# Small matmuls placed in separate row and column groups of the array, and the squares taken as the query units leave the array

## The reference

```python
for l in range(DEPTH):                                   # DEPTH = 2, 512 tokens, width 1024
    h = rms_norm(x, norm1_g[l]) * (1.0 + sc1) + sh1
    gq, gk, gv, glr, gr, sq, sk, sv, ga, gb = split(h @ w_in[l])
    ya = gla_branch(gq, gk, gv, glr, gr, ...) @ w_up_a[l]
    yb = swa_branch(sq, sk, sv, ..., rel_bias) @ w_up_b[l]
    x = x + g1 * ((sigmoid(ga) * ya + sigmoid(gb) * yb) @ w_out[l])
    ...                                                  # PEER: the larger part of the time, untouched
# gla_branch: 4 heads, chunks of 64 tokens, state S of 128 x 256 for each head
def step(S, inp):
    o = where(causal, q_dec @ k_inv.T, 0) @ v + q_dec @ S
    S = S * exp(b_last) + k_tail.T @ v
# swa_branch: 16 query heads, 2 key heads of 64, window 128
q = rms(q over 64) * qn_g / 8;  k = rms(k over 64) * kn_g
logits = q @ k.T + bias[bucket(distance)]                # then softmax with a sink, and @ v
```

## Time and profile before

| what | value |
|---|---|
| median of 3 runs | 4279.65 us |
| the profiled execution, whole | 4281.71 us |
| its span | 4279.9 us, mean granted clock of TensorE 0.967 |
| busy share: PE, DVE, POOL, ACT | 95%, 66%, 43%, 36% |
| chain that ended last | PE 77%, issue 10%, DVE 6%, ACT 3%, POOL 3%, DMA 1% |
| start, to the first unit | 0 to 62.06 us |
| GLA loop of layer 0 | 229.5 to 346.5 us |
| from its end to the head loop | 346.5 to 405.3 us |
| the same two stretches of layer 1 | 2345.3 to 2459.2 and 2459.2 to 2516.5 us |

### The profile page before, as it was taken

How to read it: one execution, slowest core, us unless ns; L and a number is a source line. 1 busy time by engine, 2 the same in 40 slices (tenths; PEclk the granted TensorE clock), 3 DMA queues, 4 the chain that set the end, 5 groups by cost and what they waited for, 6 DMA issues and landing times.

```text
span 4279.9 us, 49995 instructions
## 1 busy us (share of the span) xinstructions
PE 4056.3 (95%) x18106; PEld 3279.2 (77%) x18106; DVE 2821.2 (66%) x4282; ACT 1530.1 (36%) x2219; POOL 1845.6 (43%) x956
## 2 busy tenths in 40 slices
PE   6899998998999999999998999989899999999999
PEld 4666876886877887888876668778778778788887
DVE  3124754698988946888733156247988989378786
ACT  2434523343333333333335255233333333333332
POOL 2321223344444446777423212333344444487772
PEclk9998989999999999999999998999999999999999
DMA  6434975243445459999934358463334544699996
GB/s 246 143 116 145 329 268 201 81 143 113 170 158 201 167 206 333 382 347 349 314 127 140 103 200 301 158 194 106 125 128 179 189 159 169 239 373 372 351 350 210
DMA packets 411891, 918.72 MB, mean 215 GB/s; under 512 B 38544, under 2 KB 176560, under 8 KB 410064
## 3 DMA queue, kind: packets, MB, share of 16 engines
q1 hardware_dynamic: 328080, 664.83, 44.8%
q0 software_dynamic: 45056, 134.38, 8.6%
q10 hardware_dynamic: 38592, 117.46, 7.0%
HBM read 793.85 MB, written 256.90 MB: 246 GB/s over the span
## 4 chain that ended last, share of the span: by engine, by line
PE 77%; issue 10%; DVE 6%; ACT 3%; POOL 3%; DMA 1%; SPq 1%; POOLq 0%; ACTq 0%; DVEq 0%
PE ps L887 13%; PE ps L888 13%; PE ps L889 13%; PE ps L902 10%; PE ps L903 10%; PE ps L904 10%; POOL w_lo L841 3%; PE ps L1185 2%; PE ps L1074 1%; PE ps L1059 1%; PE ps L1019 1%; DMA raw<-in_stream_dram 1%; ACT w_hi L519 1%; DVE raw L1263 1%; PE ps L1082 1%
## 5 line engine op out<-in xcount | busy, mean ns | idle before, releaser
L841 POOL TENSOR_TENSOR w_lo<-raw,w_hi 128x1024 fp32r<-128x1024 f32 x440 | 1133.5, 2577 | 2076.0 <-ACT w_hi L519 2076.0
L519 ACT ACTIVATE w_hi<-raw 128x1024 fp32r<-128x1024 f32 x504 | 534.2, 1060 | 1873.0 <-PE ps L889 1397.2
L887 PE MATMUL ps<-h_hi,w_hi 128*128 128x512 f32 x2880 | 1146.0, 398 | 7.9 <-DVE idxT L1522 7.8
L888 PE MATMUL ps<-h_hi,w_lo 128*128 128x512 f32 x2880 | 1137.3, 395 | 0.0
L889 PE MATMUL ps<-h_lo,w_hi 128*128 128x512 f32 x2880 | 1134.8, 394 | 0.0
L887 PEld LDWEIGHTS ps<-h_hi,w_hi 128*128 128x128 f32 x2880 | 550.3, 191 | 130.7 <-issue 17.4
L889 PEld LDWEIGHTS ps<-h_lo,w_hi 128*128 128x128 f32 x2880 | 547.8, 190 | 120.1
L888 PEld LDWEIGHTS ps<-h_hi,w_lo 128*128 128x128 f32 x2880 | 549.0, 191 | 107.9
L854 POOL DMA_INDIRECT down<-expert_down,e_row x256 | 336.3, 1314 | 216.6 <-DVE ps L1647 95.9
L1594 DVE TENSOR_TENSOR hot_i<-same_i,pick 128x1024 fp32r<-128x1024 f32 x192 | 421.5, 2195 | 0.0
L846 POOL DMA_INDIRECT acts<-expert_act,e_act x256 | 375.5, 1467 | 104.1 <-issue 77.4
(11 more groups left out here) (255 smaller groups left out, 6048.2 us busy)
## 6 DMA issues: line engine op xcount, KB each, us to landing
raw<-in_stream_dram SPq DMA_DIRECT2D x648, 512.0 KB, 3.4
expert_down<-in_stream_dram SPq DMA_DIRECT2D x256, 512.0 KB, 5.9
expert_act<-gel ACTq DMA_DIRECT2D x256, 256.0 KB, 2.0
raw_more<-in_stream_dram SPq DMA_DIRECT2D x128, 512.0 KB, 6.8
expert_gate<-gatebuf ACTq DMA_DIRECT2D x12, 4096.0 KB, 12.5
a_in<-expert_act SPq DMA_DIRECT2D x128, 384.0 KB, 6.6
g_in<-expert_gate SPq DMA_DIRECT2D x128, 384.0 KB, 8.2
ada_first<-in_stream_dram SPq DMA_DIRECT2D x16, 512.0 KB, 12.6
```

What stands on the lines that cost most here:

```text
L519: return act.activation(o, i, ACT.Copy)
L841: pool.tensor_tensor(w_lo[:, s, :], raw[:, b, :], w_hi[:, s, :].bitcast(F32), ALU.subtract).then_inc(lo_ready, 1)
L887: pe.matmul(o, w_hi[:, s, w], mov_hi[:, c, :], start=c == 0, stop=False)
L888: pe.matmul(o, w_lo[:, s, w], mov_hi[:, c, :], start=False, stop=False)
```

## The change

Four edits.

1. **Bands.** `rel` and `onehot` are loaded four times, to partitions 0, 32, 64 and 96, by eight small transfers instead of two. Head h's matmul uses the 32 rows from 32 (h mod 4), and six PSUM banks instead of two.
2. **State updates.** One call now makes the products of both chunks of a tile for two heads, the even chunk on rows 0 to 63 into bank 4, the odd chunk on rows 64 to 127 into bank 5; the second call, for the other two heads, follows the first unit. There are three states instead of two, and VectorE updates both chunks before the mean squares of the output.
3. **Squares.** ScalarE takes the square of a query or key unit straight from PSUM when it copies the unit out, into six buffers. TensorE sums them inside the GLA loop, four to a bank, each into 32 partitions of its own (32 columns of the array). The reciprocal and the root follow in the last tile, on 128 partitions.
4. **Root spreads.** Each uses 32 rows and one of six banks; keys first. Four stand ahead of unit `U_MIXA + 2`, four behind it, the last two (queries of heads 12 to 15) behind `U_MIXA + 3`. `bias_free` is raised once the root is there.

```diff
+BAND_BANKS = (0, 1, 4, 5, 6, 7)
+ROOTS = (8, 9, 0, 1, 2, 3, 4, 5, 6, 7)
+ROOT_BANKS = (4, 5, 6, 7, 2, 3)
...
+    state_2 = at("state_2", 88.5, [P, GH, DV])
-    inv_rms = at("inv_rms", Z + 92, [20, SEQ])
-    spread = at("spread", Z + 98, [20, 10 * P])
+    inv_rms = at("inv_rms", Z + 110, [P, SEQ])
+    spread = at("spread", Z + 104, [P, 3, P])
+    squares = [at(f"square{b}", Z + kb, [P, SEQ]) for b, kb in enumerate((64, 66, 68, 70, 96, 110))]
...
+        def state_at(c, h):
+            return state[:, c % 3, h, :] if c % 3 < 2 else state_2[:, h, :]
...
# SyncE: the constants
-            sp.dma_start(rel[:], rel_in).then_inc(consts_loaded, 16)
-            sp.dma_start(onehot[:], onehot_in).then_inc(consts_loaded, 16)
+            for g in range(4):
+                r = slice(32 * g, 32 * g + 32)
+                sp.dma_start(rel[r], rel_in).then_inc(consts_loaded, 16)
+                sp.dma_start(onehot[r], onehot_in).then_inc(consts_loaded, 16)
...
# ScalarE
+            def square(l, m):
+                t = m - U_SQ
+                if t >= 6:
+                    act.wait_ge(sq_mm, l * 10 + t - 5)
+                act.activation(squares[t % 6][:], ps[:, ORDER[m] % 2, :], ACT.Square).then_inc(sq_ready, 1)
...
+                elif m in range(U_SQ, U_SV):
+                    square(l, m)
+                    column_out(l, m, qT_s[:, m - U_SQ, :] if m < U_SK else kT_s[:, m - U_SK, :])
...
-                transposed_hi(oa_hi, l * 2 * KC)
-                square(0)
-                for t in range(1, 10):
-                    square(t)
-                after_unit(l, U_MIXA)
                 act.wait_ge(sq_inv, l + 1)
                 act.activation(inv_rms[:], inv_rms[:], ACT.Sqrt).then_inc(sq_root, 1)
+                act.wait_ge(sq_mm, (l + 1) * 10)
+                transposed_hi(oa_hi, l * 2 * KC)
+                after_unit(l, U_MIXA)
                 after_unit(l, U_MIXA + 1)
...
# TensorE: band
             for h in range(SH):
-                if h >= 2:
-                    pe.wait_ge(band_out, h - 1)
-                pe.matmul(ps[:, h % 2, 0:384], rel[:, h:h + 1].to_broadcast([32, P]), onehot[:], start=True, stop=True
-                          ).then_inc(band_mm, 1)
+                if h >= len(BAND_BANKS):
+                    pe.wait_ge(band_out, h - len(BAND_BANKS) + 1)
+                r = slice(32 * (h % 4), 32 * (h % 4) + 32)
+                pe.matmul(ps[:, BAND_BANKS[h % len(BAND_BANKS)], 0:384], rel[r, h:h + 1].to_broadcast([32, P]), onehot[r],
+                          start=True, stop=True).then_inc(band_mm, 1)
...
# TensorE: GLA loop over p
+                def updates(l, p, half):
+                    n = l * 2 * TT + 2 * p + half
+                    if n:
+                        pe.wait_ge(state_ready, n)
+                    for h in (2 * half, 2 * half + 1):
+                        for e in range(2 if p < TT - 1 else 1):
+                            r = slice(64 * e, 64 * e + 64)
+                            mm = pe.matmul(ps[:, 4 + e, h % 2 * 256:h % 2 * 256 + 256], ktail[r, h, p, :],
+                                           v_g[r, p, h * DV:(h + 1) * DV], start=True, stop=True)
+                    mm.then_inc(upd_mm, 1)
...
-                    for e in range(2):
-                        c = 2 * p + e
-                        if e:
-                            unit(l, U_SQ + 3 * p)
-                        if c == 7:
-                            break
-                        if c:
-                            pe.wait_ge(state_ready, l * 7 + c)
-                        r = slice(64 * e, 64 * e + 64)
-                        for h in range(GH):
-                            mm = pe.matmul(ps[:, 4 + h // 2, h % 2 * 256:h % 2 * 256 + 256], ktail[r, h, p, :],
-                                           v_g[r, p, h * DV:(h + 1) * DV], start=True, stop=True)
-                        mm.then_inc(upd_mm, 1)
+                    updates(l, p, 0)
+                    unit(l, U_SQ + 3 * p)
+                    updates(l, p, 1)
                     for m in range(U_SQ + 3 * p + 1, min(U_SQ + 3 * p + 3, U_MIXA)):
                         unit(l, m)
+                    for t in range(max(4 * p - 4, 0), min(4 * p, 10)):
+                        pe.wait_ge(sq_ready, l * 10 + t + 1)
+                        r, w = 32 * (t % 4), C_HEADS + 18 - 2 * (t // 4)
+                        pe.matmul(ps[r:r + 32, 7, :], const[:, w:w + 32], squares[t % 6][:], start=t < 4, stop=t >= 6,
+                                  skip_group_check=True).then_inc(sq_mm, 1)
                     pe.wait_ge(attn_ready, k + 1)
-                    pe.wait_ge(state_ready, l * 7 + 2 * p + 1)
+                    pe.wait_ge(state_ready, l * 2 * TT + 2 * p + 2)
...
# TensorE: after the loop
-                for t in range(10):
-                    pe.wait_ge(sq_ready, l * 10 + t + 1)
-                    w = C_HEADS + 18 - 2 * t
-                    pe.matmul(ps[0:20, 2, :], const[:, w:w + 20], tmp[:, t % 2, :], start=t == 0, stop=t == 9
-                              ).then_inc(sq_mm, 1)
...
-                for t in range(10):
-                    if t >= 2:
-                        pe.wait_ge(sqk_ready, l * 10 + t - 1)
-                    pe.matmul(ps[:, 2 + t % 2, :], spread[:, t * P:t * P + P], inv_rms[:], start=True, stop=True
-                              ).then_inc(root_mm, 1)
-                pe.wait_ge(sqk_ready, (l + 1) * 10)
+                def roots(first, last):
+                    for n in range(first, last):
+                        t = ROOTS[n]
+                        if n >= 6:
+                            pe.wait_ge(sqk_ready, l * 10 + n - 5)
+                        r = slice(32 * (t % 4), 32 * (t % 4) + 32)
+                        pe.matmul(ps[:, ROOT_BANKS[n % 6], :], spread[r, t // 4, :], inv_rms[r], start=True, stop=True).then_inc(root_mm, 1)
...
+                roots(0, 4)
+                unit(l, U_MIXA + 2)
+                roots(4, 8)
+                pe.wait_ge(sqk_ready, l * 10 + 8)
                 logits(0)
-                unit(l, U_MIXA + 2)
                 unit(l, U_MIXA + 3)
+                roots(8, 10)
+                pe.wait_ge(sqk_ready, l * 10 + 10)
                 for h in range(SH):
...
# VectorE: GLA loop
+                def update(p, half):
+                    dve.wait_ge(upd_mm, l * 2 * TT + 2 * p + half + 1)
+                    if p:
+                        dve.wait_ge(o_mm, l * TT + p)
...
-                    update(2 * p)
+                    update(p, 0)
+                    update(p, 1)
+                    if p == TT - 1:
+                        dve.wait_ge(sq_mm, (l + 1) * 10)
+                        step(dve.tensor_scalar(inv_rms[:], ps[:, 7, :], EPS, None, ALU.add))
+                        dve.reciprocal(inv_rms[:], inv_rms[:]).then_inc(sq_inv, 1)
...
-                    if p < TT - 1:
-                        update(2 * p + 1)
...
# VectorE: after the loop
                 gated_a(l, 0)
-                dve.wait_ge(sqk_ready, (l + 1) * 10)
+                dve.wait_ge(sq_root, l + 1)
                 dve.sem_inc(bias_free, 1)
...
+                rooted(0, 8)
...
                     if h == 0:
+                        rooted(8, 10)
                         dve.wait_ge(silu_ready, l + 2)
```

78 lines of the change are left out of this document (34 added, 44 removed).

## The result

The changed kernel takes 4222.45 us (median of 4 runs, 4219.56 to 4226.69), the kernel before 4277.74 on the same chip (4272.71 to 4283.12): a ratio of 0.9871, 95% interval 0.9854 to 0.9888. Forecast was 4214, range 4197 to 4243. When the pair was timed again the ratio was 0.9828 (0.9794 to 0.9863); the kernel before read higher then (4295.07) and the changed one the same (4223.60).

What follows compares the result with a forecast made beforehand. TensorE, busy or waited for throughout, was taken as the bound. Start 5.0 plus 2 x (GLA loop 17 + between loops 18.0 - head loop 4.3) = 66.4 off 4281.7 gave 4215.3, by the median 4214; range 4197 to 4243.

Steps and rivals of the forecast that it cites:

- Rows side by side: Array row groups: matmuls on different row groups overlap fully, plus 0.25 us per burst.
- GLA loop: Loop of each layer: paired updates halve bursts and waits for VectorE go, 17 us less a layer.
- Between the loops: Stretch from GLA loop to head loop: 40.7 us against 58.8, 18.0 less in each layer.
- Start: Up to the first unit: bands side by side, but data lands late; 5.0 us gained, bounds -2.7 to +7.5.
- The four blocks: Start: last four blocks of `ada_first`, queued behind the band stores, land near 44 us; dot products end at 50.6.
- 5.0 of 6.3: Start: of 6.3 us, 5.0 counted, since the second `w_lo` now falls beside the norm's work.
- One is lengthened as now: Start: one VectorE dot product stretched from 1.22 to 3.37 us while GpSimd works on `w_lo` beside it.
- Head loop: Gives back 4.3 us a layer: wait of 2.7 at head 1 and 1.6 for half clock behind it.
- The chain to head 1: Head loop: late buffers, load, ScalarE's copy, table load and exponentials end 13.2 us after its begin; TensorE wants them at 10.5.
- no overlap: Rival, whole change: row groups don't overlap, nor four column groups more than now; 27 us gained, 4253; chance 0.09.
- Lateness: Rival, head loop: buffers stay late through twelve heads, 52 us a layer lost, 4309; chance 0.03.
- The ring as pace maker: Rival: weight buffers, not TensorE, tie the head loop; between the loops only 7.9 gained a layer, 4225; chance 0.12.

Runs made afterwards that it cites:

- updates alone: The kernel before with only the state-update edit (chunks paired on row groups, third state, VectorE updating both chunks ahead of the normaliser): 4244.27 us, ratio 0.9895.
- the stores moved: Changed kernel with six root spreads ahead and early dot products, plus band stores put behind all sixteen loads of `ada_first`: 4200.35 us, ratio 0.9772.
- the weights ahead of them: As the kernel with the stores moved, but band stores also behind the first four weight blocks and the parameter rows: 4206.80 us, ratio 0.9815.
- early dot products: Changed kernel with head 0's two dot products ahead of VectorE's last two multiplications by the root: 4214.14 us, ratio 0.9828.
- Six spreads ahead: Changed kernel with six root spreads in one stretch, the last four behind head 0's logits, and early dot products: 4204.08 us, ratio 0.9791.

## Why the prediction was right, and where it was not

- **Rows side by side**: right, and the size too. Forecast 1.15 for an update burst and 1.1 for one of four squares; measured 1.14 and 1.06.
- **GLA loop**: right in its size (17 against 18.7 and 15.7), incomplete in its cause. The prediction put the end of the waits down to the new pairing ("the products of p wait only for the update of p - 1"). The runs split layer 0 so: 11.8 from moving VectorE's update ahead of the normaliser (move alone); 10.5 from pairing on rows with what was left of the waits (105.2 to 94.7, updates alone); 3.5 back for the squares (94.7 to 98.2). In layer 1: 10.2, 9.1 and 3.5. Taken in this sequence, over half of the gross gain is an order on VectorE that needs no row groups. It stands in the diff, and I walked past it, because I priced without asking what VectorE did in the 2.6 us. The split depends on the sequence: with the squares in the loop and no pairing the same move was worth 17.3 and 11.7 (123.9 and 118.9 against 106.6 and 107.2), and the pairing without the move was not run. That the size came out near is in part luck: tile 0 gained 4.9 (2.5 forecast) and tile 3 2.7 (3.8 forecast).
- **Between the loops**: right, 17.9 and 18.0 against 18.0, and term by term in layer 0: the first four spreads 1.99 (1.9 forecast), the next four with the wait 3.9 (4.0), head 0's logits and the unit behind them 10.6 (10.3), the last two spreads with theirs 2.6 (2.5).
- **Start**: a mis-sized term, 2.8 against 5.0. Its mechanism (data, then one stretched dot product) holds: VectorE waits 5.5 for data, and 3.6 us are gone with the stores behind the loads. Two sizes were off. The four blocks were there at 45.2 and not near 44, so the dot products end at 52.0 instead of 50.6. And the prediction took 5.0 of 6.3 on the ground that the second `w_lo` would fall beside the norm; it fell beside the tiny operation ahead of the norm and stretched that from 0.17 to 2.19. "One is lengthened as now" misreads the kernel before, where two were; the 56.9 that it is compared with holds both.
- **Head loop**: the step was right and the size about half of what it is, 4.3 against 9.8 and 6.6. Forecast for head 1 was a wait of 2.7 and 1.6 of half clock behind it. In layer 0 the wait was 3.45 and the half clock behind it 1.5; another 1.6 of half clock stands ahead of it, between head 1 and head 2, behind the waits of 2.80 and 1.49. I priced those two waits, and their half clock only up to head 1. In layer 1 the two waits brought nothing there (clock 1.00 from head 1 to head 2), but the wait was 4.84 and the half clock behind it 2.6. That is 6.6 of the 9.8 in layer 0, and 7.4, more than all of the 6.6, in layer 1. The chain to head 1 was 14.9 in layer 0 and not 13.2: the buffer came free 2.2 after the loop's begin (2.3 forecast), the load took 7.0 (6.0), the copy 1.1, and the table load with the exponentials and the copy behind them 4.6. The 3.8 forecast for these last was an estimate that no row stood behind.
- **What stays open**: the rest of 3 us. In every kernel some later heads take up to 5.5 us longer than 9.7, and which ones changes from kernel to kernel and from one execution of the changed kernel to another. The traces show more than that. From head 3 to head 12 the long steps all lead from an odd head's logits to an even head's, and each holds a wait of TensorE for `pT`, ScalarE's copy of the probabilities. In each of them ScalarE is idle for 2.9 to 8.5 us before its copy of the weights, and then has two table loads and the sigmoid of a gate between that copy and the exponentials. The longest in the changed kernel, head 9 to head 10 of layer 0, takes 15.2 us at a clock of 0.78:

```profile
445.61 1.06 ACT L530 ACTIVATE w_hi<-raw 128x1024 fp32r<-128x1024 f32 x1 [8.52 <-DMA raw<-in_stream_dram]
...
453.20 1.73 PE L1093 MATMUL ps<-const,logit 128*128 128x128 f32 x7 [2.67 <-ACT pT L530]
```

  No run changed this, and why it is this head and not another was not tried. Head loops with nothing late ahead of them took 130.2 to 134.6 over five kernels in both layers, but with the stores moved 133.2 and 143.1, and with the weights ahead of them 143.6 and 138.0. So of a gain below some 5 us the end of the kernel may show nothing.
- **The rivals**: no overlap is excluded by the bursts. Lateness heals: behind head 3 the step is 9.6 to 9.8 for the next heads, but for one of 10.1. The ring as pace maker cannot be excluded by the time: its 4225 is nearer the measured 4222.45 than my 4214, and from the end of the GLA loop to the last head's logits the changed kernel gained 8.1 in layer 0 and 11.3 in layer 1, where that rival says 7.9 and I said 13.7. What speaks against it is the table above: the last head does not move with head 0's dot products, and between the long steps TensorE is busy throughout. With the dot products held back in the kernel before it was the same: 9 us later, and the last head 5.7 later. So late buffers are a cause of the give-back (3.4 us in layer 0 by the run with early dot products) and of single long steps, but they do not set the pace of the loop.

Two sums of the prediction are off by a little, without changing what follows: the ring rival's 405.3 less 18.0 plus 2.3 is 389.6 and not 389.3, and 4279.65 less 66.4 is 4213 and not 4214.

The edits add up. Bands 0.999, updates 0.9895 and squares with roots 0.9964 multiply to 0.985; the changed kernel read 0.9871 and 0.9828. Six spreads ahead with the stores moved has the lowest median measured: 23 us under the changed kernel, of which 19.5 are the spreads. The last 4 are told from nothing by the first unit (54.89 against 58.46), not by the times, whose ranges overlap.

## What to carry to other kernels

When a change lets one engine stop waiting, look at what the other engine did just before it delivered: here a small operation with a wait of its own stood ahead of the update, and moving the update ahead of it gave over half of the loop's gain. Where a change adds a wait for another engine, price the half clock behind it too, over the whole stretch to the next long run of work. A total inside the range does not say which of two mechanisms is at work: here a rival's number lay nearer, and only runs that moved one cause at a time told them apart. A gain at the start has to be followed to the end: each of the first moves only brought the next chain up.

## What the runs showed of the hardware

- Four matmuls in a burst ran equally fast with the row halves alternating and with two and two: 1.14 us both.
- A VectorE operation with both inputs in SBUF was stretched beside GpSimd's `w_lo` by the same time at two sizes: 128x1024 from 1.22 to 3.37, and 128x16 from 0.18 to 2.19. One `w_lo` mostly takes 2.35 to 2.45 undisturbed (two in 4.67 at the start of the kernel with the stores moved), and two beside VectorE took 6.57. The Trainium skill (SBUF — State Buffer, SBUF: two separate sides) says that the two hold a shared port pair for a whole instruction, and the other is blocked; the trace agrees, since operations that differ 64 times in size lose the same 2.0 to 2.15 us.
- Behind idle times of 2.80 and 1.49 us the granted clock did not always fall alike. In the next 8.1 to 11.3 us, all busy, it was 0.70 in both layers of the kernel with early dot products (3.2 us lost), 0.82 in layer 0 of the changed kernel (1.6 lost) and 1.00 in its layer 1. With these waits gone, head 1 to head 3 ran at 1.00 in both layers, in spite of idle times of 1.13 and 1.80 there; with the stores moved as well it was 1.00 and 0.92.
